# Forgetting bias of attention scores: fp32 products replaced by single-pass products of a rounded part and a rest, tables on Pool

## The chip, the cores and the metric

The kernel runs on one core of a Trainium2 chip. The metric is the device time of one launch in microseconds (us), the median of several runs. Every run computes the whole reference from inputs in HBM to outputs in HBM.

## The reference

One inference step of a two-layer encoder for 256 prompt tokens and 32 sample tokens, width 1024. Each layer is a SwiGLU block, a combined projection `z = h @ w_in` whose columns feed three head groups (forgetting attention, RWKV-7 mixing, retention), an output projection, a second SwiGLU block and a gated addition. The change touches forgetting attention (8 heads of 64):

```
c = cumsum(logf)                       # per head; for the sample over 512 cached + 32 new tokens
s = q k^T * 64**-0.5 + c[query] - c[key]
p = softmax(mask(s));  o = p v
```

The term `c[query] - c[key]` is the forgetting bias. It has to be exact to fp32 level, since the cached `logf` are large.

## The kernel before

All activations are feature-major (128 partitions are features, the free dimension is the 288 tokens). Weights come as 1 MB slots through a ring of four. Large products are made of operands split in two: a rounded part (type fp32r, made by ACT with a copy) and a rest (made by DVE with a subtraction, L844 and L930), and three single-pass products hi·hi, hi·lo, lo·hi. Small products in the mixers stay in fp32, which the trace records as two matmul records each.

There is one hand-written order per engine, joined by counting semaphores. In a layer: the first SwiGLU block; the z projection, 31 blocks of 24 products (`z_block`, L1465), for which ACT makes the rounded part (`z_cast`, L566) and DVE the rest (`z_rest`, L930) and the eviction of the block two before (`z_evict`, L939); `z_next(n)` is eviction n-2 and rest n. Between the z_next calls DVE does the small elementwise work of the mixers, in program order. Then come triangular solves and retention, and then attention and the RWKV recurrence interleaved: nine steps of the recurrence (L1769, L1775, L1782, with DVE's L1206 and L1213) and between them the attention of four head pairs (`fox_scores`, `fox_weights`, `fox_products`, `fox_back`). The sample's attention, the output projection and the second SwiGLU block follow.

The forgetting bias is part of the score product, as one more product into the same PSUM bank: `foxL` (weights, 128 rows x one column per head and query) times `foxR` (moving, 128 rows x 800 keys: 256 prompt, 512 cached, 32 new). Rows 0 to 7 of foxL hold 8·c of the query at the row of its head and rows 0 to 7 of foxR hold ones; rows 32 to 39 of foxL hold -8 at the row of the head (loaded once, L346) and rows 32 to 39 of foxR hold c of all keys; all other rows are zero. `fox_scores` (L1701) issues four such products per head pair, of 128 and 256 columns, and L1835 four for the sample, of 512 and 32 columns.

DVE makes c by scans over 8 partitions (L1057, L1058, L1060, multiplier: the ones of foxR), copies it to foxR (L1062, 8x800), and behind z_next(22) writes 8·c into foxL: one product of 8x2048 (L1064) and two of 8x128 (L1067), with broadcast operands. POOL issues loads of states and caches and stores of results, and makes a few elementwise products of RWKV's output stage (L440 to L443, L459, L460) while DVE works beside it. `cbuf`, where c stands, shares its memory with `tok`, which ACT writes after z (L644).

Of the kernel before, what the change touches and what calls it, by code (L numbers as in the profile page):

```python
# [19 lines left out]
F32 = mybir.dt.float32  # L20
# [59 lines left out]
for _name, _n in (("n1", DB), ("nm", DB), ("n2", DB), ("pn", DB), ("mu", 7), ("prev", 7), ("bf", 1), ("w0", 2),  # L80
# [27 lines left out]
    gn_ps=8, gn_sq=2, gn_ln=4, gn_rs=2, rot_ps=4, rotd=4, decd=2, rtr_ps=3, rtrc=3, sm_ps=6, smd=6, kv_ps=5,  # L108
    rsd=10, ro_ps=2, ro_ok=3, rgate=2, fu_ok=1, fl_ok=1, lgf_ok=1, fc_ok=3, vt_ps=3, vtc=3, fs_ps=8, fmx=16,
    fexp=16, ft_ps=8, ftc=8, fo_ps=4, fno=4, ft2=4, fo_ok=4, ss_ps=2, smx=2, sexp=4, st_ps=4, stc=4, so_ps=1,  # L110
# [19 lines left out]
def program(nc, wcol, x_in, p_in, consts_in, params_in, foxl_in, kc_in, vc_in, clf_in, srwkv_in, sret_in,  # L130
            nf_in, y_out, k_out, v_out, logf_out, shift_out, rwkv_out, ret_out):
    with ExitStack() as ctx:
        def sb(name, *shape):
            return ctx.enter_context(nc.sbuf_tensor(name, list(shape), F32))
# [18 lines left out]
        nf = sb("nf", P, DB)  # L153
        foxL = sb("foxL", P, FOX_H * T)
        foxLp = foxL[:, 0:FOX_H * TP].rearrange("p (h t) -> p h t", h=FOX_H)
        foxLs = foxL[:, FOX_H * TP:]
        foxR = sb("foxR", P, TP + PAST + TS)
        et = sb("et", P, 2, T)
# [170 lines left out]
        with nc.Block() as block:  # L329
            @block.sync  # L330
            def _(sp):
# [12 lines left out]
                sp.dma_start(nf[:], nf_in).then_inc(start_sem, 16)  # L344
                sp.wait_ge(clear_sem, 2)
                sp.dma_start(foxL[32:40, :], foxl_in).then_inc(start_sem, 16)  # L346

            @block.gpsimd
            def _(pool):
                pool.memset(foxL[:], 0.0).then_inc(clear_sem, 1)  # L350
                pool.memset(foxR[:], 0.0).then_inc(clear_sem, 1)
                pool.wait_ge(clear_sem, 2)
                pool.memset(foxR[0:8, :], 1.0).then_inc(clear_sem, 1)

# [9 lines left out]
        with nc.Block() as block:  # L364
# [41 lines left out]
            @block.gpsimd  # L406
            def _(pool):
                for layer in range(DEPTH):
                    past = counted(layer)
# [12 lines left out]
                    pool.dma_start(rst[:, 0, :, :], sret_in[layer, 0]).then_inc(S["ret_in"], 16)  # L422
                    pool.dma_start(rst[:, 5, :, :], sret_in[layer, 1]).then_inc(S["ret_in"], 16)

                    pool.wait_ge(S["z_ev"], past["z_ev"] + Z_BANKS + NZ)
# [41 lines left out]
            def _(act):  # L467
                n_chain = [0]
                for layer in range(DEPTH):
# [87 lines left out]
                    if layer == 0:  # L557
                        act.wait_ge(start_sem, 64)
                    def z_cast(n):
# [78 lines left out]

                    act.wait_ge(S["zstore"], layer * ZSTORE_PER_LAYER + 16)
                    for j in range(3):  # L640
                        n = TILES[j][1]
                        for k in range(2):
                            act.wait_ge(S["tr_ps"], past["tr_ps"] + 2 * j + k + 1)
                            act.activation(tok[0:n, j, 4 * k:4 * k + 4, :].rearrange("p a b -> p (a b)"),  # L644
                                           bank[6 + k][0:n, :], ACT.Copy).then_inc(S["trc"], 1)
# [171 lines left out]
            def _(dve):  # L817
                n_chain = [0]
                for layer in range(DEPTH):
                    past = counted(layer)  # L820

                    def link(ins):

                        n_chain[0] += 1
                        ins.then_inc(S["vchain"], 1)
                        dve.wait_ge(S["vchain"], n_chain[0])
# [94 lines left out]
                    if layer == 0:  # L921
                        dve.wait_ge(start_sem, 64)

# [125 lines left out]
                    for b in range(2):  # L1049
# [3 lines left out]
                    dve.wait_ge(S["mixin"], layer * MIXIN_PER_LAYER + 48)  # L1053
                    w = con[e8, CONSTS["fox8"][0]:CONSTS["fox8"][0] + 8]
                    unit = foxR[e8, :]
                    z_next(20)
# [4 lines left out]
                                                cbuf[e8, TP + PAST - 1:TP + PAST], ALU.mult, ALU.add))  # L1061
                    link(dve.tensor_copy(foxR[32:40, :], cbuf[e8, :]))  # L1062
                    z_next(22)
                    dve.tensor_tensor(foxLp[e8], cbuf[e8, 0:TP].unsqueeze(1).to_broadcast([8, FOX_H, TP]),  # L1064
                                      w.unsqueeze(2).to_broadcast([8, FOX_H, TP]), ALU.mult).then_inc(S["fc_ok"], 1)
                    for g in range(2):
                        dve.tensor_tensor(foxLs[e8, 128 * g:128 * g + 128].rearrange("p (b t) -> p b t", b=4),  # L1067
                                          cbuf[e8, TP + PAST:].unsqueeze(1).to_broadcast([8, 4, TS]),
                                          w.rearrange("p (b g) -> p g b", g=2)[:, g, :].unsqueeze(2).to_broadcast([8, 4, TS]),
                                          ALU.mult).then_inc(S["fc_ok"], 1)  # L1070
                    z_next(23)
# [270 lines left out]
            def _(pe):  # L1342
                for layer in range(DEPTH):
# [107 lines left out]
                    if layer == 0:  # L1451
                        pe.wait_ge(start_sem, 64)
                    def z_block(n):
# [237 lines left out]
                    pe.wait_ge(S["uac"], past["uac"] + 8)  # L1691
                    pe.wait_ge(S["fc_ok"], past["fc_ok"] + 3)

# [235 lines left out]
def constants():  # L1929
# [52 lines left out]
    put("dchunk", np.concatenate([np.exp(lg * 64.0), np.exp(lg * TS)], 1))  # L1982
    put("fox8", 8.0 * np.eye(8))
    cols = np.zeros((P, 8))
# [158 lines left out]
```

## Time and profile before

| | us |
|---|---|
| median of 3 runs | 1439.85 (1438.88 to 1444.85) |
| profiled execution | 1437.9 |
| its span | 1436.1 |
| PE busy in it | 1367.6 |
| DVE busy | 864.2 |
| ACT busy | 597.0 |
| POOL busy | 49.3 |

The profile is of one execution; the span is from its first to its last instruction. PE's matmul records overlap (the length of one is its latency, 0.29 us for 288 columns, while a new one starts every 0.13 us), so lengths of groups of them are read from one group's start to the next one's. Lines beginning with a time are of the timeline: start in us, duration in us, engine, line, operation, output<-inputs, shape, and how many were merged. The mean granted clock of TensorE over the span was 0.968 of 2.4 GHz.

### The profile page before, as it was taken

The numbers are of one execution on the slowest core, as the hardware profiler recorded it, in microseconds if no ns is written. First come the engines' busy times: TensorE is split into PE (matmuls) and PEld (weight loads), VectorE is DVE, ScalarE is ACT, GpSimd is POOL, SyncE is SP. The second block draws the span as 40 slices with busy tenths as digits, with TensorE's granted clock in tenths as the row PEclk, the third lists the DMA queues.
The fourth block names the chain that finished last, engine by engine and source line by source line (L and its number), as shares of the span: only waits on it lengthen the run. The fifth ranks groups of instructions, "written<-read, shape, count | busy, mean of one in ns | idle before, by whom it ended". The sixth has DMA issues, their size and how long they took to land.

```text
span 1436.1 us, 29222 instructions
## 1 busy us (share of the span) xinstructions
PE 1367.6 (95%) x12544; PEld 1317.7 (92%) x12544; DVE 864.2 (60%) x1365; ACT 597.0 (42%) x845; POOL 49.3 (3%) x71
## 2 busy tenths in 40 slices
PE   6999999998898999999999999999989899999997
PEld 6999999898777999999989999998977699999996
DVE  5766536796346566653766664467853565766546
ACT  5443434533326544433544343335333364443333
POOL 1000000003100000000000000000031100000000
PEclk9999999999779999999999999999997899999999
DMA  8444443434103344444444444523432035444440
GB/s 315 166 175 157 165 171 122 147 122 152 65 14 118 147 162 160 175 154 169 151 151 176 154 168 173 178 90 120 163 110 64 14 118 199 153 175 156 167 146 34
DMA packets 31328, 205.29 MB, mean 143 GB/s; under 512 B 4312, under 2 KB 5864, under 8 KB 7544
## 3 DMA queue, kind: packets, MB, share of 16 engines
q1 hardware_dynamic: 28672, 195.62, 37.9%
q0 software_dynamic: 2560, 8.26, 1.7%
q8 instruction: 75, 1.23, 0.3%
q14 instruction: 21, 0.17, 0.0%
HBM read 199.77 MB, written 4.10 MB: 142 GB/s over the span
## 4 chain that ended last, share of the span: by engine, by line
PE 88%; DVE 4%; ACT 4%; issue 2%; DMA 1%; POOL 0%; SPq 0%; DVEq 0%; ACTq 0%
PE banks L1390 40%; PE banks L1413 19%; PE banks L1465 11%; PE banks L1919 3%; PE banks L1882 3%; PE banks L1887 1%; PE banks L1701 1%; PE banks L1900 1%; PE banks L1743 1%; PE banks L1643 1%; PE banks L1821 1%; PE banks L1706 1%; ACT split_h L572 1%; PE banks L1631 1%; PE banks L1731 0%
## 5 line engine op out<-in xcount | busy, mean ns | idle before, releaser
L1390 PE MATMUL banks<-split_x,split_w 128*128 128x288 f32 x4224 | 570.5, 297 | 16.2 <-ACT split_x L492 11.8
L1390 PEld LDWEIGHTS banks<-split_x,split_w 128*128 128x128 f32 x4224 | 567.4, 190 | 18.8 <-issue 11.7
L844 DVE TENSOR_TENSOR split_w<-wc,split_w 128x2048 fp32r<-128x2048 f32 x139 | 318.6, 2292 | 346.5 <-ACT split_w L508 346.5
L508 ACT ACTIVATE split_w<-wc 128x2048 fp32r<-128x2048 f32 x139 | 266.4, 1916 | 401.0 <-PE banks L1390 207.4
L1413 PE MATMUL banks<-split_x,split_w 128*128 (+1 forms) x2112 | 282.3, 295 | 0.0
L1413 PEld LDWEIGHTS banks<-split_x,split_w 128*128 128x128 f32 x2112 | 281.8, 188 | 0.0
L1465 PE MATMUL banks<-split_h,split_x 128*128 128x288 f32 x752 | 115.7, 301 | 5.7 <-ACT split_x L566 4.2
L1465 PEld LDWEIGHTS banks<-split_h,split_x 128*128 128x128 f32 x752 | 105.9, 191 | 9.0 <-DVE zT L939 5.4
L566 ACT ACTIVATE split_x<-wc 128x1024 fp32r<-128x1024 f32 x62 | 65.1, 1057 | 112.2 <-PE banks L1465 97.2
L533 ACT ACTIVATE et<-hT 128x288 f32<-128x288 f32 x88 | 35.5, 445 | 110.4 <-DVE hT L863 110.3
L1465 PE MATMUL banks<-split_x 128*128 128x288 f32 x496 | 76.9, 298 | 0.0
L1465 PEld LDWEIGHTS banks<-split_x 128*128 128x128 f32 x496 | 70.2, 191 | 0.0
L1919 PE MATMUL banks<-split_x,split_w 128*128 128x288 f32 x384 | 53.0, 297 | 0.0
L1919 PEld LDWEIGHTS banks<-split_x,split_w 128*128 128x128 f32 x384 | 51.7, 189 | 1.1 <-ACT split_x L784 1.1
L939 DVE TENSOR_TENSOR zT<-banks,rs 128x288 f32<-128x288 f32 x62 | 28.1, 454 | 33.0 <-PE banks L1465 24.1
L1465 PE MATMUL banks<-split_h,split_e 128*128 128x288 f32 x240 | 38.2, 302 | 7.5 <-DVE split_e L930 7.5
L868 DVE SCALAR_TENSOR_TENSOR et<-et,hT 128x288 f32<-128x288 f32 x88 | 36.4, 455 | 12.6 <-ACT et L533 9.1
L930 DVE TENSOR_TENSOR split_x<-wc,split_x 128x1024 fp32r<-128x1024 f32 x32 | 39.0, 1218 | 7.8 <-ACT split_x L566 7.8
L874 DVE SCALAR_TENSOR_TENSOR et<-et,banks 128x288 f32<-128x288 f32 x88 | 39.3, 450 | 4.8 <-PE banks L1390 3.5
L1465 PEld LDWEIGHTS banks<-split_h,split_e 128*128 128x128 f32 x240 | 34.4, 193 | 8.4 <-DVE split_e L930 8.4
L930 DVE TENSOR_TENSOR split_e<-wc,split_x 128x1024 fp32r<-128x1024 f32 x30 | 36.5, 1217 | 6.8 <-ACT split_x L566 6.8
L863 DVE TENSOR_TENSOR hT<-banks,rs 128x288 f32<-128x288 f32 x88 | 35.9, 449 | 5.9 <-ACT rs L487 5.9
(290 smaller groups left out, 1194.6 us busy)
## 6 DMA issues: line engine op xcount, KB each, us to landing
wc<-wcol SPq DMA_DIRECT2D x182, 1024.0 KB, 4.8
arena<-kc_in POOLq DMA_DIRECT2D x8, 256.0 KB, 3.5
arena<-vc_in POOLq DMA_DIRECT2D x2, 1024.0 KB, 7.5
con<-consts_in SPq DMA_DIRECT2D x1, 1830.0 KB
xT<-x_in SPq DMA_DIRECT2D x2, 576.0 KB, 4.5
k_out<-zT POOLq DMA_DIRECT2D x8, 144.0 KB, 2.5
v_out<-zT POOLq DMA_DIRECT2D x8, 144.0 KB, 2.5
y_out<-hT SPq DMA_DIRECT2D x8, 144.0 KB, 1.9
```

The lines of the kernel that those rows point to most:

```text
L508: act.activation(ws[(s + 1 - f) % 2][0], wc[:, p % RING, :], ACT.Copy).then_inc(S["cast"], 1)
L566: act.activation(zw[n % 2][0], z_raw(n), ACT.Copy).then_inc(S["zcast"], 1)
L844: dve.tensor_tensor(lo, wc[:, (POS_FFN[f] + s) % RING, :], hi, ALU.subtract).then_inc(S["wlo"], 1)
L863: dve.tensor_tensor(half[:, q % 2, :], bank[2 * (q % 4)][:, 0:T], rs[:], ALU.mult)\
L868: dve.scalar_tensor_tensor(e, e, 1.0, half[:, q % 2, :], ALU.add, ALU.mult)\
L874: dve.scalar_tensor_tensor(e, e, 0.5, bank[2 * (q % 4) + 1][:, 0:T], ALU.mult, ALU.mult)\
L930: dve.tensor_tensor(lo, z_raw(n), hi, ALU.subtract).then_inc(S["zlo"], 1)
L1390: mm = pe.matmul(o, w[:, k, cs], x[:, k, :], start=(n == 0 and k == 0), stop=(n == 2 and k == DB - 1))
L1413: return pe.matmul(bank[m][:, 0:T], w[:, kk, m * 128:m * 128 + 128], rhs, start=start, stop=stop)
L1465: mm = pe.matmul(o, w[:, k, :], zh_lo(k) if second else zh_hi[:, k, :], start=(i == 0 and k == 0), stop=(i == 2 and k == DB - 1))
L1882: pe.matmul(bank[2 * s + cc][:, 0:T], hi[:, k, cc * 128:cc * 128 + 128], x[:, k, :], start=(x is oh_hi and k == 4), stop=False)
L1919: mm = pe.matmul(bank[2 * s + cc][:, 0:T], w[:, k, cc * 128:cc * 128 + 128], x[:, k, :], start=(n == 0 and k == 0), stop=(n == 2 and k == ...
```

## The change

c is split like the weights: a rounded part and a rest, both fp32r. foxL and foxR become fp32r tensors, so that the products on L1701 and L1835 are single-pass. Rows 0 to 7 and 64 to 71 of foxR hold the rounded part and the rest of c, against rows 0 to 7 and 64 to 71 of foxL with -8; rows 32 to 39 and 96 to 103 of foxR hold ones, against the rounded part and the rest times 8 in foxL. The number of products and their shapes stay.

DVE: the scans' multiplier is a broadcast constant column. The copy to foxR ahead of z_next(22) and the three products behind it go; in their place behind z_next(22) stand the rounding copy to foxR, the subtraction for the rest, and two copies of the parts to rows 32 and 96 of cbuf. POOL makes the tables of foxL from these, in two sets of one 8x2048 and two 8x128 products, between its loads of retention states and its stores of k and v; in the first launch part it also copies the -8 rows from a staging place to foxL after all constants are loaded.

```
-                sp.wait_ge(clear_sem, 2)
-                sp.dma_start(foxL[32:40, :], foxl_in).then_inc(start_sem, 16)
+                for r in (0, 64):
+                    sp.dma_start(extra[r:r + 8, 0:FOX_H * T], foxl_in).then_inc(start_sem, 16)
...
-                pool.memset(foxR[0:8, :], 1.0).then_inc(clear_sem, 1)
+                for r in (32, 96):
+                    pool.memset(foxR[r:r + 8, :].bitcast(F32), 1.0).then_inc(clear_sem, 1)
...
+                pool.wait_ge(start_sem, 80)
+                pool.wait_ge(clear_sem, 4)
+                for r in (0, 64):
+                    pool.tensor_copy(foxL[r:r + 8, :], extra[r:r + 8, 0:FOX_H * T]).then_inc(clear_sem, 1)
+                pool.wait_ge(clear_sem, 6)
...
+                    for i, r in enumerate((32, 96)):
+                        rows = slice(r, r + 8)
+                        w = c("fox8", rows)
+                        pool.wait_ge(S["fr_ok"], past["fr_ok"] + 3 + i)
+                        pool.tensor_tensor(foxLp[rows], cbuf[rows, 0:TP].unsqueeze(1).to_broadcast([8, FOX_H, TP]),
+                                           w.unsqueeze(2).to_broadcast([8, FOX_H, TP]), ALU.mult).then_inc(S["fc_ok"], 1)
+                        for g in range(2):
+                            pool.tensor_tensor(foxLs[rows, 128 * g:128 * g + 128].rearrange("p (b t) -> p b t", b=4),
+                                               cbuf[rows, TP + PAST:].unsqueeze(1).to_broadcast([8, 4, TS]),
+                                               w.rearrange("p (b g) -> p g b", g=2)[:, g, :].unsqueeze(2).to_broadcast([8, 4, TS]),
+                                               ALU.mult).then_inc(S["fc_ok"], 1)
+                    pool.wait_ge(S["fc_ok"], past["fc_ok"] + 6)
...
                     act.wait_ge(S["zstore"], layer * ZSTORE_PER_LAYER + 16)
+                    act.wait_ge(S["fc_ok"], past["fc_ok"] + 6)
...
-                    unit = foxR[e8, :]
+                    unit = col(C_ONE, e8).to_broadcast([8, PAST])
...
-                    link(dve.tensor_copy(foxR[32:40, :], cbuf[e8, :]))
                     z_next(22)
-                    dve.tensor_tensor(foxLp[e8], ...
-                    for g in range(2):
-                        dve.tensor_tensor(foxLs[e8, 128 * g:128 * g + 128]...
+                    dve.tensor_copy(foxR[e8, :], cbuf[e8, :]).then_inc(S["fr_ok"], 1)
+                    dve.wait_ge(S["fr_ok"], past["fr_ok"] + 1)
+                    dve.tensor_tensor(foxR[64:72, :], cbuf[e8, :], foxR[e8, :], ALU.subtract).then_inc(S["fr_ok"], 1)
+                    dve.tensor_copy(cbuf[32:40, :], foxR[e8, :]).then_inc(S["fr_ok"], 1)
+                    dve.wait_ge(S["fr_ok"], past["fr_ok"] + 2)
+                    dve.tensor_copy(cbuf[96:104, :], foxR[64:72, :]).then_inc(S["fr_ok"], 1)
                     z_next(23)
...
-                    pe.wait_ge(S["fc_ok"], past["fc_ok"] + 3)
+                    pe.wait_ge(S["fr_ok"], past["fr_ok"] + 2)
+                    pe.wait_ge(S["fc_ok"], past["fc_ok"] + 6)
```

The waits on the start semaphore count to 80 in place of 64, and the constant `fox8` stands at rows 32 and 96.

## Rows read from the trace of the kernel before

**Rows 1.** The page: busy times of the engines, and the chain's shares by engine.
```profile
PE 1367.6 (95%) x12544; PEld 1317.7 (92%) x12544; DVE 864.2 (60%) x1365; ACT 597.0 (42%) x845; POOL 49.3 (3%) x71
...
PE 88%; DVE 4%; ACT 4%; issue 2%; DMA 1%; POOL 0%; SPq 0%; DVEq 0%; ACTq 0%
```
**Rows 2.** Timeline of PE, z stage of layer 0.
```profile
314.14 1.23 PE L1465 MATMUL banks<-split_h,split_e 128*128 128x288 f32 x8
...
317.34 1.23 PE L1465 MATMUL banks<-split_h,split_x 128*128 128x288 f32 x8
...
323.17 1.32 PE L1465 MATMUL banks<-split_h,split_e 128*128 128x288 f32 x8 [1.52 <-DVE split_e L930]
```
**Rows 3.** Timeline of DVE, the same stretch.
```profile
306.44 0.57 DVE L1062 COPY foxR<-extra 8x800 f32<-8x800 f32 x1
...
308.55 2.27 DVE L1064 TENSOR_TENSOR foxL<-extra,con 8x2048 f32<-8x2048 f32 x1
...
310.75 0.47 DVE L1067 TENSOR_TENSOR foxL<-extra,con 8x128 f32<-8x128 f32 x2
...
311.52 1.20 DVE L930 TENSOR_TENSOR split_e<-wc,split_x 128x1024 fp32r<-128x1024 f32 x1
...
314.16 0.76 DVE L1081 TENSOR_TENSOR zT<-zT,et 128x576 f32<-128x576 f32 x1
```
**Rows 4.** Timeline of POOL over the span.
```profile
2.68 0.76 POOL L351 MEMSET foxR<- 128x800 f32 x1
3.51 0.75 POOL L353 MEMSET foxR<- 8x800 f32 x1
...
348.40 1.68 POOL L441 TENSOR_TENSOR arena<-arena 128x576 f32<-128x576 f32 x1
...
433.98 1.40 POOL L459 TENSOR_TENSOR arena<-arena 128x576 f32<-128x576 f32 x1 [8.21 <-ACT arena L728]
```
**Rows 5.** Lines 1114 and 1115: ns min/median/max, first and last start in us.
```profile
L1114 DVE TENSOR_TENSOR hT<-zT,con x2: 744/748/751, 348.1 to 1059.3; 128x576 f32<-128x576 f32 x2
...
L1115 DVE TENSOR_TENSOR hT<-zT,con x2: 1949/1956/1964, 348.8 to 1060.0; 128x576 f32<-128x576 f32 x2
```
**Rows 6.** Chain of waits in layer 0's attention: start us, us, what.
```profile
378.24 2.86 PE banks L1701 x8
...
388.27 1.31 PE banks L1701 x8
...
395.21 0.66 PE banks L1731 x6
...
405.33 1.28 PE banks L1731 x6
406.61 2.56 PE banks L1701 x8
...
429.05 2.54 PE banks L1835 x8
```
**Rows 7.** Windows of 2 us: length, PE busy (records), clock, DMA share, GB/s.
```profile
380.00:382.00 2.00, 2.00 (x10) 0.50 0.94 371
382.00:384.00 2.00, 1.80 (x30) 0.99 0.18 72
```
**Rows 8.** z stages: PE timeline and windows (layer 1); PE waits, whole-stage window (0).
```profile
944.11 1.30 PE L1465 MATMUL banks<-split_h,split_x 128*128 128x288 f32 x8 [2.10 <-ACT split_x L566]
...
944.00:946.00 2.00, 1.89 (x12) 0.81 0.00 0
946.00:948.00 2.00, 2.00 (x10) 0.50 0.28 49
948.00:950.00 2.00, 2.00 (x15) 0.83 0.84 336
...
PE banks L1465 <- DVE split_e L930: 3.8, 2, 2.2
...
204.00:342.00 138.00, 130.78 (x995) 127.07 (x998) 97.51 (x147) 59.16 (x85) 2.69 (x5) 1.00 0.41 146
```

More of the change, by code:

```diff
@@ L108 @@
     gn_ps=8, gn_sq=2, gn_ln=4, gn_rs=2, rot_ps=4, rotd=4, decd=2, rtr_ps=3, rtrc=3, sm_ps=6, smd=6, kv_ps=5,
-    rsd=10, ro_ps=2, ro_ok=3, rgate=2, fu_ok=1, fl_ok=1, lgf_ok=1, fc_ok=3, vt_ps=3, vtc=3, fs_ps=8, fmx=16,
+    rsd=10, ro_ps=2, ro_ok=3, rgate=2, fu_ok=1, fl_ok=1, lgf_ok=1, fr_ok=4, fc_ok=6, vt_ps=3, vtc=3, fs_ps=8, fmx=16,
     fexp=16, ft_ps=8, ftc=8, fo_ps=4, fno=4, ft2=4, fo_ok=4, ss_ps=2, smx=2, sexp=4, st_ps=4, stc=4, so_ps=1,
@@ L153, in program @@
         nf = sb("nf", P, DB)
-        foxL = sb("foxL", P, FOX_H * T)
+        foxL = ctx.enter_context(nc.sbuf_tensor("foxL", [P, FOX_H * T], F32R))
         foxLp = foxL[:, 0:FOX_H * TP].rearrange("p (h t) -> p h t", h=FOX_H)
         foxLs = foxL[:, FOX_H * TP:]
-        foxR = sb("foxR", P, TP + PAST + TS)
+        foxR = ctx.enter_context(nc.sbuf_tensor("foxR", [P, TP + PAST + TS], F32R))
         et = sb("et", P, 2, T)
@@ L344, in _ @@
                 sp.dma_start(nf[:], nf_in).then_inc(start_sem, 16)
-                sp.wait_ge(clear_sem, 2)
-                sp.dma_start(foxL[32:40, :], foxl_in).then_inc(start_sem, 16)
+                for r in (0, 64):
+                    sp.dma_start(extra[r:r + 8, 0:FOX_H * T], foxl_in).then_inc(start_sem, 16)
             @block.gpsimd
             def _(pool):
-                pool.memset(foxL[:], 0.0).then_inc(clear_sem, 1)
-                pool.memset(foxR[:], 0.0).then_inc(clear_sem, 1)
+                pool.memset(foxL[:].bitcast(F32), 0.0).then_inc(clear_sem, 1)
+                pool.memset(foxR[:].bitcast(F32), 0.0).then_inc(clear_sem, 1)
                 pool.wait_ge(clear_sem, 2)
-                pool.memset(foxR[0:8, :], 1.0).then_inc(clear_sem, 1)
+                for r in (32, 96):
+                    pool.memset(foxR[r:r + 8, :].bitcast(F32), 1.0).then_inc(clear_sem, 1)
             @block.scalar
@@ L557, in _ @@
                     if layer == 0:
-                        act.wait_ge(start_sem, 64)
+                        act.wait_ge(start_sem, 80)
                     def z_cast(n):
@@ L921, in _ @@
                     if layer == 0:
-                        dve.wait_ge(start_sem, 64)
+                        dve.wait_ge(start_sem, 80)
+                        dve.wait_ge(clear_sem, 6)
                     def z_rest(n):
@@ L1053, in _ @@
                     dve.wait_ge(S["mixin"], layer * MIXIN_PER_LAYER + 48)
-                    w = con[e8, CONSTS["fox8"][0]:CONSTS["fox8"][0] + 8]
-                    unit = foxR[e8, :]
+                    unit = col(C_ONE, e8).to_broadcast([8, PAST])
                     z_next(20)
@@ L1061, in _ @@
                                                 cbuf[e8, TP + PAST - 1:TP + PAST], ALU.mult, ALU.add))
-                    link(dve.tensor_copy(foxR[32:40, :], cbuf[e8, :]))
                     z_next(22)
-                    dve.tensor_tensor(foxLp[e8], cbuf[e8, 0:TP].unsqueeze(1).to_broadcast([8, FOX_H, TP]),
-                                      w.unsqueeze(2).to_broadcast([8, FOX_H, TP]), ALU.mult).then_inc(S["fc_ok"], 1)
-                    for g in range(2):
[L1067 to L1070, printed above, removed]
+                    dve.tensor_copy(foxR[e8, :], cbuf[e8, :]).then_inc(S["fr_ok"], 1)
[4 more added lines that the diff above has]
+                    dve.tensor_copy(cbuf[96:104, :], foxR[64:72, :]).then_inc(S["fr_ok"], 1)
                     z_next(23)
@@ L1451, in _ @@
                     if layer == 0:
-                        pe.wait_ge(start_sem, 64)
+                        pe.wait_ge(start_sem, 80)
                     def z_block(n):
@@ L1982, in constants @@
     put("dchunk", np.concatenate([np.exp(lg * 64.0), np.exp(lg * TS)], 1))
-    put("fox8", 8.0 * np.eye(8))
+    fox8 = np.zeros((P, 8))
+    fox8[32:40] = fox8[96:104] = 8.0 * np.eye(8)
+    put("fox8", fox8)
     cols = np.zeros((P, 8))
```

## The prediction

> **What bounds the kernel now.** I read the page's busy shares and its chain first. The reader is to see that PE is busy 95% of the span and carries 88% of the chain that ended last [rows 1]: time is won or lost where PE's stream shortens or has to wait. The change touches three stretches of each layer, so the second view is the timeline there: PE and DVE in the z projection (one block of 24 products per 3.2 us, 314.14 to 317.34), where DVE makes the rests that PE consumes [rows 2, 3]; the 36 us in which POOL works beside DVE [rows 4, 5]; and the attention stretch from 378 us, where every group of fox products is a link of the chain [rows 6]. The last view is the granted clock by windows of 2 us [rows 7, 8], because the attention stretch runs at 1.2 and at 2.4 GHz by turns.
>
> **Scores on PE.** Four groups of four fp32 products per layer become four groups of four single-pass ones. A product of 128 or 256 columns is now two records. At full clock a group takes 1.31 us; at half clock 2.86 and 2.56 us [rows 6]. Single-pass records of 128x128 (the transposes) take 0.66 / 6 = 0.11 us at full clock and 1.28 / 6 = 0.21 us at half [rows 6]. So a new group costs about 4 x 0.11 to 0.12 = 0.47 us at full and 0.88 us at half. Per layer this removes 2 x 0.84 (groups two and three) + 1.98 + 1.68 = 5.3 us. The sample's products, 2.54 us partly at half clock [rows 6], have 2 x (512 + 32) columns; the two wide ones become 2 x 0.23 us by the z products' rate (3.2 us / 24 = 0.133 us for 288 columns [rows 2], in proportion), the narrow ones 0.11 each: 0.7 us, so 1.5 us less on the mean of the layers (less where the clock is full). Together 6.8 us a layer. What follows is late instead: after the second group PE meets ACT's copies and DVE's maxima, which start only when the scores are there and move along with them, but not all; I take 85%, 5.8 us a layer, 11.6 us in both. Bounds: nothing on records that are narrower than 288 columns, if the single pass needs wide operands, to the full 13.6 us.
>
> **Clock of that stretch.** The clock came back to 2.4 GHz at 382 us, right behind the first score group and the products after it, and it is at half through 380 to 382 although PE was busy all the time [rows 7]; by the fourth group, at 406.61 us, it had fallen again, since that took 2.56 us where the second took 1.31 [rows 6]. The dense four-pass products are what stands ahead of the rise. With a quarter of their array time the rise may come later or not at all, and the fall sooner. By the transposes' 0.66 against 1.28 us [rows 6], PE's own work doubles; of the some 30 us of the stretch that have full clock, PE would lose up to 10 us in a layer (a third; the rest is overhead, waits and the other engines). Ends: 0 and 10 us a layer. I take the middle, 5 us a layer, 10 us in all, since the trace shows no such stretch without the dense products. The Trainium skill (TensorE: Matmul & The Clock Gate, Part 4: PE-mode transpose) says that transposes do not count as PE work for the clock. No row here separates them; by that rule it would be the transposes that cannot stand in for the scores, and the loss would be the upper end, 20 us.
>
> **DVE in the z stage.** Removed behind z_next(22): 2.27 + 0.47 us, and the copy of 0.57 us ahead of it [rows 3]. Added: three copies of 8x800 at 0.57 us and a subtraction of 800 columns at 2.27 / 2048 = 1.11 ns each, 0.89 us: 2.6 us against 3.3. Were the rounding copy at one column per such step, 0.3 us more. DVE is not late by this: rest(23), which ended at 312.72 us (311.52 + 1.20 [rows 3]), is needed by PE at 314.14 us [rows 2]. The scan's multiplier becomes a repeated constant column: no price either way. Alone this part is worth 0.
>
> **The tables on POOL, and what they hold up.** POOL gets, twice per layer, one product of 8x2048 and two of 8x128. POOL's 128x576 product with nobody in its way took 1.40 us; a memset of 8x800 took as long as one of 128x800, 0.75 and 0.76 us [rows 4], so few partitions don't help. Less some 0.1 us of start, that is 2.26 ns a column, 4.7 us for 2048, 0.4 us for 128. By 1.40 / 576 it would be 5.0 us. The Trainium skill (GPSIMD Engine Reference, 3.1 Elementwise) gives 4.5 us for 2048 columns; the sum would be 0.4 us a layer lower. POOL's deadline is far (PE reads the tables at 378 us, ACT overwrites their source behind z), so its own time costs nothing. What it does to DVE does. L1114 and L1115 are the same operation, 128x576 with two operands in SBUF: 0.75 us and 1.95 us, in both layers [rows 5]. The second met POOL's L441, 348.40 to 350.08 us [rows 4], started at 348.8 us and ended 0.62 us behind it, at 350.70. So a DVE operation with two SBUF operands stood still until POOL's two-operand product was through. DVE's rests (L930) are of that kind.
>
> Layer 0 in the new order (times from the rows of the stage, [rows 2, 3]): scan to 306.4, z_next(22) to 308.1, round 308.7, subtract 309.65, copy 310.25 (this frees POOL), copy 310.85, POOL's first long product 310.9 to 315.5. DVE's eviction reads one operand from PSUM and goes on; rest(23) waits and ends at 315.5 + 1.1 = 316.6. PE wants it at 314.14: 2.4 us of stall. POOL's short ones and DVE's L1078, L1079 interleave to about 318.1; the second long product takes 318.1 to 322.8 and holds L1081; the eviction, a short POOL product and rest(24) follow, to 325.1 us. PE wants rest(24) at 317.34 + 2.4 = 319.75: 5.4 us of stall. The stall of 1.52 us before 323.17 stays, since it hangs on the rotation behind block 24 [rows 2]. Sum 7.8 us per layer, 15.6 us in all. Lower bound 0 (operations on 8 partitions may not hold DVE), upper 2 x 10 us (slower POOL product for the repeated operands). Idle PE also costs clock: behind a gap of 2.10 us in layer 1's z stage three windows show 0.81, 0.50 and 0.83, which is (0.19 + 0.50 + 0.17) x 2 / 0.5 = 3.4 us at half, while layer 0 had two waits of that size (3.8 us together) and kept 1.00 [rows 8]. A gap of 5.4 us I expect to cost one such spell per layer, 1.7 us, 3.4 us in all (0 to 7).
>
> **Cheap edits.** Start: one memset more (0.75 us [rows 4]) and one DMA more on SP, whose wait for the memsets goes; both end inside the 9 us until the first weights are there. The copies of 8x2304 on POOL come after the constants have landed, some 20 us in, and could hold DVE's rest of 2.3 us per weight slot for 2 to 5 us each; DVE is busy 60% [rows 1], so I take 0, and 2 us if PE waits for one. They also stand ahead of POOL's loads of states and cached gates, which are needed 280 us later. New waits: ACT's for the tables is behind z, 15 us after they are ready; POOL's stands ahead of the stores of k and v, whose data come last in z; PE's is met. 0.
>
> **Sum.** Against the profiled execution, 1437.9 us: + 15.6 (stalls) + 3.4 (clock there) - 11.6 (scores) + 10 (clock in attention) = 1455.3 us. The median of the runs shown, 1439.85, lies 2 us higher: 1457 us.
>
> **Rivals.** (1) POOL holds DVE, but the clock in attention stays as it is: 1439.85 + 15.6 + 1.7 - 11.6 = 1445.6 us, hardly to be told from before. For it: the clock kept 1.00 through other stretches of small products; against: both rises stand behind score groups. (2) POOL doesn't hold DVE, because it touches 8 partitions: then the gain stands, 1439.85 - 11.6 = 1428 us, or 1438 us with half of the clock lost; this is the one on the other side. It decides if rest(23) and L1081 keep 1.20 and 0.76 us beside POOL. For it: no row shows an 8-partition product beside DVE; against: L1115 in both layers. (3) Both losses at their full size, clock at half through attention: 1439.85 + 15.6 + 3.4 - 11.6 + 20 = 1467 us. (4) The single pass isn't one at 128 and 256 columns: the gain is 3 us (the sample's wide products alone) instead of 11.6, but the clock in attention stays: 1439.85 + 15.6 + 3.4 - 3 = 1456 us. Every single-pass product of this trace has 288 columns, which neither speaks for it nor against.
>
> **Chances.** Forecast 0.43 (own range 1448 to 1466), rival one 0.20, two 0.25, three 0.08, four 0.04. Within 0.5% of 1439.85 (1432.7 to 1447.0) is about what measurement can't tell from no change. Slower: all of three and four, nearly all of the forecast and a quarter of rival one, 0.58. Same: most of rival one and the part of rival two with clock lost, 0.27. Faster: 0.15. The range reaches from rival two's middle to rival three, 1432 to 1468 us.
>
> **What would show it.** POOL's long products should take 4.5 to 5 us; rest(23) and L1081 5 us instead of about 1; PE should show two waits for L930 or L1081 of 2 to 6 us in each z stage, followed by a half-clock window; score groups of 4 records in 0.5 us; fewer full-clock windows from 378 to 420 us. I am wrong if DVE's operations beside POOL keep their lengths, or if the attention stretch keeps its clock and the net falls under 1447 us.

## The result and the profile after

| | before | after |
|---|---|---|
| median of 4 runs each, us | 1439.76 (1438.88 to 1444.85) | 1454.68 (1450.57 to 1460.71) |
| profiled execution, us | 1437.9 | 1450.57 |
| its span | 1436.1 | 1449.0 |
| PE busy | 1367.6 | 1376.7 |
| PE records | 12544 | 12504 |
| granted clock | 0.968 | 0.952 |

The ratio is 1.0087, 95% interval 1.0055 to 1.0119: slower by 0.9%, 2.3 us less than forecast. Timed a second time, beside other kernels, the changed kernel had 1.0075 (1.0047 to 1.0102). Ratios leave out slow runs, those more than 1.5% above the fastest of their kernel: one of 6 in that second timing, one of 12 with memsets (whose profile is of that run), 4 of 12 with filler in the gaps. PE is busy 9 us longer with fewer records, which is the first sign of a lower clock. From the page of the profile after: busy times, chain shares, and a group of DVE's rests, whose mean of 1413 ns hides long ones:

```profile
PE 1376.7 (95%) x12504; PEld 1326.7 (92%) x12504; DVE 876.5 (60%) x1365; ACT 597.6 (41%) x845; POOL 77.7 (5%) x86
...
PE 87%; DVE 6%; ACT 3%; issue 2%; DMA 1%; POOL 0%; SPq 0%; DVEq 0%; ACTq 0%; POOLq 0%
...
L951 DVE TENSOR_TENSOR split_e<-wc,split_x 128x1024 fp32r<-128x1024 f32 x30 | 42.4, 1413 | 6.8 <-ACT split_x L585 6.8
```

The z stage of layer 0. POOL's timeline (start us, us, engine, line, operation, shape, count, idle before it):

```profile
313.50 3.97 POOL L435 TENSOR_TENSOR foxL<-extra,con 8x2048 fp32r<-8x2048 f32 x1 [3.44 <-DVE extra L1086]
317.45 1.73 POOL L438 TENSOR_TENSOR foxL<-extra,con 8x128 fp32r<-8x128 f32 x2
319.25 4.17 POOL L435 TENSOR_TENSOR foxL<-extra,con 8x2048 fp32r<-8x2048 f32 x1
323.39 1.28 POOL L438 TENSOR_TENSOR foxL<-extra,con 8x128 fp32r<-8x128 f32 x2
```

DVE beside it; L951 and L1099 answer to L930 and L1081 of [rows 3]:

```profile
311.24 0.56 DVE L1083 CAST foxR<-extra 8x800 fp32r<-8x800 f32 x1
311.83 0.98 DVE L1085 TENSOR_TENSOR foxR<-extra,foxR 8x800 fp32r<-8x800 f32 x1
...
314.05 0.46 DVE L960 TENSOR_TENSOR zT<-banks,rs 128x288 f32<-128x288 f32 x1
314.42 4.14 DVE L951 TENSOR_TENSOR split_e<-wc,split_x 128x1024 fp32r<-128x1024 f32 x1
...
319.21 0.74 DVE L1097 TENSOR_TENSOR zT<-zT,con 128x576 f32<-128x576 f32 x1
319.99 4.05 DVE L1099 TENSOR_TENSOR zT<-zT,et 128x576 f32<-128x576 f32 x1
...
324.45 1.30 DVE L951 TENSOR_TENSOR split_x<-wc,split_x 128x1024 fp32r<-128x1024 f32 x1
```

The rest that took 1.20 us in [rows 3] takes 4.14, and L1081's 0.76 has become 4.05. Each ends about its own length behind POOL's long product: 318.56 against 317.47, 324.04 against 323.42. The eviction of 0.46 us, which reads one operand from PSUM, ran beside the same product at its own length. So did L1097, 0.74 us, with two operands in SBUF: it started 0.04 us before the second long product, so it had come first. The waits that this makes on PE, from PE's timeline:

```profile
318.61 1.32 PE L1483 MATMUL banks<-split_h,split_e 128*128 128x288 f32 x8 [1.16 <-DVE split_e L951]
325.80 1.42 PE L1483 MATMUL banks<-split_h,split_x 128*128 128x288 f32 x8 [3.74 <-DVE split_x L951]
332.78 1.32 PE L1483 MATMUL banks<-split_h,split_e 128*128 128x288 f32 x8 [0.95 <-DVE split_e L951]
```

And windows behind the longest of these waits (us, PE busy, PEld busy, DVE, ACT, POOL, clock, DMA share, GB/s):

```profile
326.00:328.00 2.00, 2.00 (x11) 1.71 (x11) 0.00 (x0) 0.69 (x1) 0.00 (x0) 0.71 0.03 8
328.00:330.00 2.00, 2.00 (x8) 1.71 (x7) 1.28 (x3) 0.36 (x1) 0.00 (x0) 0.50 0.00 0
330.00:332.00 2.00, 1.83 (x13) 1.59 (x11) 1.93 (x4) 0.00 (x0) 0.00 (x0) 0.93 0.00 0
```

The attention stretch of layer 0: the chain of the profile after, whose groups of 4 records answer to those of 8 in [rows 6]:

```profile
388.12 1.15 PE banks L1720 x4
...
398.69 0.85 PE banks L1720 x4
...
408.11 1.28 PE banks L1750 x6
409.39 0.85 PE banks L1720 x4
...
420.69 0.85 PE banks L1720 x4
...
440.39 0.59 PE banks L1854 x4
```

Groups two to four are as short as promised for half clock; the first takes 1.15 us. But the transposes beside the third group take 1.28 us where the ones at full clock took 0.66, and none of the four groups ran at full clock throughout (in layer 1 the second did). Windows of 72 us over this stretch, before and then after; the clock, third from the end, falls from 0.83 to 0.67:

```profile
378.00:450.00 72.00, 62.80 (x780) 49.80 (x777) 36.58 (x106) 28.98 (x69) 4.41 (x5) 0.83 0.11 38
```

```profile
388.00:460.00 72.00, 66.15 (x757) 53.83 (x754) 36.11 (x106) 29.36 (x69) 4.42 (x5) 0.67 0.10 33
```

Both profiled executions were laid side by side between fixed points of PE's stream. "Half" is the time at 1.2 GHz in the stretch.

| stretch | layer 0 before | after | layer 1 before | after |
|---|---|---|---|---|
| z block 22 to block 26 | 15.52 (half 0) | 21.98 (3.4) | 15.53 (0) | 21.78 (3.4) |
| first scores to end of recurrence | 37.19 (10.7) | 40.03 (31.0) | 37.35 (10.9) | 37.25 (21.2) |
| on to the sample's products | 13.49 (9.2) | 11.94 (6.8) | 8.11 (0) | 7.54 (0) |
| on to the output projection | 14.41 (1.0) | 13.53 (7.2) | 14.08 (4.2) | 13.14 (6.0) |

z: +6.5 and +6.3, 12.7 us. Attention: +0.4 and -1.6, -1.2 us. The first z product starts 1.6 us later (226.44 before, 227.99 after); kernels below with the same start have 226.4 to 227.4, so at least half of this is scatter. Other stretches nearly cancel: blocks 0 to 21 of z +1.6 and -1.6 us (a half-clock spell more in one layer, one less in the other), the stretch ahead of the first scores +0.3 and -1.8, and all behind the attention +1.4. Sum 13.0; the span grew by 12.9.

### The profile page after: what moved, and what is told of

Read it like the earlier page. It is cut to its first block, busy times and chain, and to the rows that moved or that the text cites. A ratio compares the mean times of both kernels' runs of the same rounds, so it can differ in the third digit from the quotient of the medians.

```text
span 1449.0 us, 29161 instructions
## 1 busy us (share of the span) xinstructions
PE 1376.7 (95%) x12504; PEld 1326.7 (92%) x12504; DVE 876.5 (60%) x1365; ACT 597.6 (41%) x845; POOL 77.7 (5%) x86
## 4 chain that ended last, share of the span: by engine, by line
PE 87%; DVE 6%; ACT 3%; issue 2%; DMA 1%; POOL 0%; SPq 0%; DVEq 0%; ACTq 0%; POOLq 0%
PE banks L1408 39%; PE banks L1431 19%; PE banks L1483 9%; PE banks L1938 3%; PE banks L1901 3%; PE banks L1906 1%; PE banks L1919 1%; PE banks L1762 1%; DVE split_e L951 1%; PE banks L1725 1%; DVE split_x L951 1%; DVE zT L1099 1%; PE banks L1661 1%; PE banks L1840 1%; PE banks L1788 1%
## 5 line engine op out<-in xcount | busy, mean ns | idle before, releaser
L1408 PE MATMUL banks<-split_x,split_w 128*128 128x288 f32 x4224 | 571.6, 298 | 16.7 <-ACT split_x L511 12.3
L1483 PEld LDWEIGHTS banks<-split_h,split_x 128*128 128x128 f32 x752 | 107.4, 194 | 17.4 <-DVE split_x L951 9.4
L951 DVE TENSOR_TENSOR split_e<-wc,split_x 128x1024 fp32r<-128x1024 f32 x30 | 42.4, 1413 | 6.8 <-ACT split_x L585 6.8
L951 DVE TENSOR_TENSOR split_x<-wc,split_x 128x1024 fp32r<-128x1024 f32 x32 | 39.2, 1224 | 7.9 <-ACT split_x L585 7.8
```

Source lines behind the costliest of these rows:

```text
L951: dve.tensor_tensor(lo, z_raw(n), hi, ALU.subtract).then_inc(S["zlo"], 1)
L1408: mm = pe.matmul(o, w[:, k, cs], x[:, k, :], start=(n == 0 and k == 0), stop=(n == 2 and k == DB - 1))
L1483: mm = pe.matmul(o, w[:, k, :], zh_lo(k) if second else zh_hi[:, k, :], start=(i == 0 and k == 0), stop=(i == 2 and k == DB - 1))
```

## Experiments

Ratios are to the kernel before, timed beside it on the same chip, with 95% intervals. One number is used throughout beside the time: **half-clock time** = (1 - mean granted clock) x 2 x span, mean over the runs that the ratio uses. The kernel before has 99 to 106 us of it in its timings, the changed one 148 (4 runs) and 138 (second timing, 5 runs). It scatters: over the 12 runs of one kernel it reached from 124 to 183 us, so that a mean over 12 has a standard error of 3 to 6 us. "First stretch of attention" is the second stretch of the table above, in the one profiled execution of a kernel.

**The tables on DVE, late in z.**

```
-POOL: two sets of one 8x2048 and two 8x128 products
+                        if n > 26:                 # DVE, behind z_next(27) to z_next(30)
+                            table((32, 32, 96, 96)[n - 27], (0, 4, 0, 4)[n - 27])   # 8x1024 each
+                    table_s(32); table_s(96)       # 8x128, before the last evictions
```

> The changed kernel with the tables of foxL made by DVE in place of POOL, in four products of 8x1024 behind z_next(27) to z_next(30) and four of 8x128 before the last evictions, where DVE has idle time. Theory (POOL's two-operand products hold DVE's two-operand ones in the z stage, and the rest of the change about cancels): blocks 22 to 26 of z take 15.5 us again instead of 21.8, rest(23) 1.2 us, the attention stretch as in the changed kernel, 1438 to 1442 us. Rival (the loss comes from the clock of the attention stretch): blocks 22 to 26 may recover, but the time stays at 1450 us or more.

1442.48 us against 1442.66, ratio 0.9996 (0.9964 to 1.0028). The z stretch is back at 15.52 us in both layers. Its table products on DVE, and the rests beside them:

```profile
329.33 1.22 DVE L939 TENSOR_TENSOR split_e<-wc,split_x 128x1024 fp32r<-128x1024 f32 x1
330.58 1.22 DVE L1094 TENSOR_TENSOR foxL<-extra,con 8x1024 fp32r<-8x1024 f32 x1
...
332.32 1.22 DVE L939 TENSOR_TENSOR split_x<-wc,split_x 128x1024 fp32r<-128x1024 f32 x1
```

This is the theory's result, 0.5 us above its range. DVE can do all of this work for nothing, and with it on POOL the kernel loses 0.8 to 0.9%. It also shows what the single-pass scores alone are worth: nothing, though PE has less to do. Half-clock time is 146 us, 40 more than before. The first stretch of attention took 37.3 us (half 21.3) and 39.7 (30.3).

**POOL's long product in eight pieces.**

```
+                        for h in range(FOX_H):
+                            pool.tensor_tensor(foxLp[rows, h, :], cbuf[rows, 0:TP],
+                                               w[:, h:h + 1].to_broadcast([8, TP]), ALU.mult)...
```

> The changed kernel with POOL's product of 8x2048 cut into eight of 8x256, one per head. Theory (a DVE operation stands still until the POOL product that is running is through, and gets in before the next one): no DVE operation waits more than 0.7 us, rest(23) takes 1.2 to 1.9 us, blocks 22 to 26 of z take 15.5 to 17 us, 1440 to 1444 us. Rival (POOL's reads and DVE's share the port's rate, so the sum of POOL's work counts): blocks 22 to 26 stay near 21.8 us, 1452 to 1456 us.

1442.53 us, ratio 1.0004 (0.9984 to 1.0024); z stretch 16.18 and 17.10 us. POOL, then DVE:

```profile
312.55 8.11 POOL L436 TENSOR_TENSOR foxL<-extra,con 8x256 fp32r<-8x256 f32 x8 [3.42 <-DVE extra L1087]
```

```profile
313.48 1.21 DVE L952 TENSOR_TENSOR split_e<-wc,split_x 128x1024 fp32r<-128x1024 f32 x1
...
315.34 1.01 DVE L1098 TENSOR_TENSOR zT<-zT,con 128x576 f32<-128x576 f32 x1
316.38 1.05 DVE L1100 TENSOR_TENSOR zT<-zT,et 128x576 f32<-128x576 f32 x1
```

POOL works twice as long (8.11 us where one product took 3.97), on the same data, and DVE loses at most 0.4 us per operation (0.3 in the lines shown). Blocks 22 to 26 came out 0.1 us above the theory's range in layer 1. The hold is by instruction, not by amount of traffic. It goes both ways. Two of POOL's pieces, one beside DVE's next rest and the next one alone:

```profile
317.84 1.21 DVE L952 TENSOR_TENSOR split_x<-wc,split_x 128x1024 fp32r<-128x1024 f32 x1
317.87 1.66 POOL L436 TENSOR_TENSOR foxL<-extra,con 8x256 fp32r<-8x256 f32 x1
...
319.49 0.60 POOL L436 TENSOR_TENSOR foxL<-extra,con 8x256 fp32r<-8x256 f32 x1
```

The rest, which started 0.03 us earlier, keeps its 1.21 us, and the piece ends 0.47 us behind it. So most of the added time of POOL is its waiting for DVE: alone, eight pieces would take 4.8 us (8 x 0.60, an estimate). What the cutting leaves of the loss in z, 0.7 and 1.6 us, is within the interval of the ratio.

**POOL's products replaced by memsets of the same places**, from which the query's part of the bias is missing.

```
-                        pool.tensor_tensor(foxLp[rows], cbuf[rows, 0:TP]... , ALU.mult)
+                        pool.memset(foxL[rows, :].bitcast(F32), 0.0)     # twice, then foxLs
```

> The changed kernel with POOL's products for foxL replaced by memsets of 8x2304 and 8x256 (twice 2.0 us and 0.3 us per set), so the query's part of the bias is left out. Theory (only a POOL operation that reads SBUF holds DVE's second operand): rest(23) and L1099's operation keep 1.2 and 0.76 us beside POOL, blocks 22 to 26 take 15.5 us, 1438 to 1442 us. Rival (any POOL work on SBUF holds DVE): rest(23) takes 2 to 4 us, blocks 22 to 26 17 to 20 us, 1443 to 1450 us.

1443.57 us, ratio 1.0001 (0.9975 to 1.0027); z stretch 16.54 and 16.52 us, where the theory had 15.5. POOL and DVE:

```profile
312.87 2.02 POOL L434 MEMSET foxL<- 8x2304 f32 x1 [3.54 <-DVE extra L1083]
314.95 2.34 POOL L436 MEMSET foxL<- 8x2304 f32 x1
```

```profile
312.85 2.48 DVE L1085 COPY extra<-foxR 8x800 f32<-8x800 f32 x1
...
315.73 1.22 DVE L948 TENSOR_TENSOR split_e<-wc,split_x 128x1024 fp32r<-128x1024 f32 x1
```

The rest beside a memset keeps 1.22 us; DVE's plain copy beside the first memset takes 2.48 us instead of 0.57 and ends 0.44 us behind it. The theory had left this copy out; it pushes the rests behind it back, and z is 1 us longer. The Trainium skill (SBUF — State Buffer, "Who interferes with whom") states both sides: a DVE instruction with two SBUF inputs contends with a GpSimd instruction that reads, not with one that only writes, while a copy in a two-port mode contends with either, and who comes first holds the shared ports for its whole instruction. The four pairs here agree: 4.14 us beside a product, 1.22 beside a memset, 2.48 for a copy beside a memset, 0.46 for an operation with one operand in PSUM beside a product. On who comes first, L1097 and the rest beside POOL's piece agree, each the earlier by 0.03 to 0.04 us; the copy held by the memset has the earlier start in the trace, by 0.02 us, which is too close to tell.

**The change with fp32 tables and scores**, all else as changed.

```
-        foxL = ctx.enter_context(nc.sbuf_tensor("foxL", [P, FOX_H * T], F32R))
+        foxL = sb("foxL", P, FOX_H * T)              # foxR likewise
```

> The changed kernel with foxL and foxR in fp32, so that the products stay fp32 ones (the rounded part is then all of c, the rest zero), all else as in the change. Theory: blocks 22 to 26 still take 21 to 22 us, the attention stretch is as before with 1.31 us per score group at full clock, and half-clock time there near 11 us a layer: 1453 to 1458 us. Rival (the single-pass products and their clock cost the time): 1440 to 1444 us.

1457.63 us, ratio 1.0096 (1.0071 to 1.0121). z is again 22.5 us, and the first stretch of attention 37.13 us (half 10.6) and 38.45 (12.5), as before the change. The clock of the attention stretch thus follows the kind of the score products, not the tables on POOL or the stalls in z.

**Less work still: no query part, no tables at all** (the query part left out, the copies and the waits too).

```
-                    dve.tensor_copy(cbuf[32:40, :], foxR[e8, :])...
-                    dve.tensor_copy(cbuf[96:104, :], foxR[64:72, :])...
-                    (POOL's products and the waits on them)
```

> The changed kernel without the query's part of the bias: no tables, neither on POOL nor on DVE, and without the two copies to rows 32 and 96, so the bias is -c of the key alone (the query's part is constant along a row of the softmax). Theory: blocks 22 to 26 take 15.5 us, as with late tables, attention as there, 1438 to 1443 us; the tables' DVE time was hidden. Rival (DVE's 6 us of late tables cost something at the end of z): 2 to 5 us faster than the version with late tables.

1441.81 us, ratio 1.0003 (0.9979 to 1.0028), half-clock time 139 us, z stretch 15.51 us: not the 2 to 5 us less of the rival. Whatever makes the tables, single-pass scores alone bring nothing.

**The changed kernel again.**

> The changed kernel itself once more, beside the others on the same chip. Theory: blocks 22 to 26 of z take 21 to 22 us in both layers, 1453 to 1458 us, 0.9 to 1.0% above the kernel before. Rival (the first measurement was high by the spread of the clock): 1446 to 1450 us.

1454.47 us, ratio 1.0075 (1.0047 to 1.0102). z stretch 22.43 and 22.53 us. First stretch of attention: 37.37 us (half 21.4) and 36.06 (19.0), against 40.03 (31.0) and 37.25 (21.2) in the first profile: the clock there is not the same from run to run.

**Filler in the first score group** (tables on DVE): its 128x256 single-pass product issued 7 times per head.

```
-                            for q, k1, at in parts:
+                            for q, k1, at in (7 if p == 0 else 1) * parts[1:] + parts[:1]:
```

> The version with late DVE tables, and in the first score group of each layer the 128x256 product of each head is issued seven times in place of once (twelve more products, each starting the sum anew, so the result is the same). Theory (dense products ahead of a rise bring the clock back, and the single-pass scores lack that density): the clock rises within 4 us of the first group, half-clock time from there to the end of the recurrence falls from 21 to 30 us to 11 to 17, and the stretch, 2.5 us of added products included, takes 36 to 37 us instead of 37.3 to 39.7; total 1438 to 1442 us. Rival (the clock follows something else, or the phase alone): half-clock time stays at 21 us or more, the stretch gets 2.5 us longer, total 1444 to 1450 us.

1442.69 us median (one of 12 runs took 2600.61, which nothing here explains), ratio 0.9999 (0.9981 to 1.0017). First stretch of attention 37.2 us in both layers with 16.7 half, the group 3.40 us long. It bought clock, half-clock time 125 instead of the 139 of the kernel without tables beside it, and paid as much for it: the time came out a little above the theory's range, the ratio at 1.

**Filler in the gaps** (tables on DVE): three unused 128x256 products ahead of each wait of PE in the recurrence.

```
+                        for _ in range(3):
+                            pe.matmul(bank[2][:, 256:512], foxLp[:, 0, 0:128], foxR[:, 0:256], ...)
```

> The version with late DVE tables, and in each of the nine recurrence steps three 128x256 single-pass products into unused columns of PSUM stand ahead of PE's wait for DVE's update, where PE idles some 0.2 to 0.6 us. Theory (what raises the clock and holds it is the density of PE's array work): half-clock time from the first scores to the end of the recurrence falls under 10 us per layer and the stretch takes 35 to 37 us instead of 37.3 to 39.7; total 1434 to 1440 us. Rival (the clock does not follow it): half-clock time stays above 20 us, the stretch gets up to 4 us longer, total 1446 to 1450 us.

1443.37 us is the median of all 12 runs (1426.97 to 1459.61), above the 1441.34 of the kernel before; the ratio, 0.9964 (0.9933 to 0.9994), is of 8 of them. In the profile layer 0 had 32.1 us of half clock in the first stretch of attention and layer 1 had 9.5. Inconclusive.

**Which dense group matters.** The tables on DVE; chosen score groups read the same rounded tables as fp32, the rest single-pass. Three kernels, `p == 0`, `p in (0, 3)` and `p == 3`:

```
+                                lhs, rhs = foxLp[:, 2 * p + e, q:q + 128], foxR[:, 0:k1]
+                                if p in (0, 3):
+                                    lhs, rhs = lhs.bitcast(F32), rhs.bitcast(F32)
```

> The tables are made by DVE late in z, and the first score group of each layer reads the same rounded tables as fp32 (8 records), the other three and the sample's as single-pass products. Theory (the dense four-pass products of the first group bring the clock's rise): half-clock time from the first scores to the end of the recurrence back at 10 to 13 us a layer, as with all four groups in fp32, where one with four single-pass groups has 21 to 30; the second and third groups take 0.7 us at full clock; that stretch 34 to 36 us instead of 37.2, time 1434 to 1439 us where before has 1441 (ratio 0.995 to 0.998). Rival (the rise and fall do not hang on that group): half-clock time 20 to 31 us in at least one layer, stretch 37 to 40 us, ratio 0.998 to 1.002.

> As the last, but the first and the fourth score group of each layer in fp32, the second and third and the sample's single-pass. Theory (dense products keep the clock up): half-clock time 8 to 12 us a layer, stretch from the first scores to the end of the recurrence 34.5 to 36.5 us, ratio 0.995 to 0.999. Rival (they do not): half-clock time 20 us or more in a layer, the fourth group adds 1.6 us at half clock, ratio 0.999 to 1.003.

> The tables on DVE late in z, all score groups single-pass, timed beside the two others. Theory: 0.998 to 1.001 of before as in its first run (0.9996), with half-clock time of 20 to 30 us a layer; the ratio lies above that of the kernel with its first group in fp32. Rival: all three kernels within 0.1% of each other.

> Tables on DVE late in z; of the four score groups of a layer only the fourth in fp32. Half-clock time is counted as (1 - granted clock) x 2 x span, mean over the timed runs: 106 us for the kernel before, 146 with four single-pass groups, 135 with only the first in fp32, 108 with the first and the fourth. Theory one (the fourth group, where the clock falls, is what decides): half-clock time 105 to 120 us, ratio 0.993 to 0.997. Theory two (both are needed: the clock follows the work of the whole stretch): 125 to 140 us, ratio 0.998 to 1.002. Rival (any fp32 group only costs its own array time and the clock is scatter): 146 us as with none, ratio 1.001 to 1.003.

| groups in fp32 | median us (before beside it) | ratio | half-clock time | half clock in first stretch of attention, layers 0 and 1 of the profile |
|---|---|---|---|---|
| none | 1443.20 (1442.86) | 0.9999 (0.9972 to 1.0026) | 145 | 39.7, 35.3 (first profile 21.3, 30.3) |
| first | 1442.87 (1442.86) | 1.0010 (0.9983 to 1.0038) | 135 | 8.3, 16.2 |
| fourth | 1442.11 (1442.13) | 0.9990 (0.9966 to 1.0013) | 133 | 28.6, 30.9 |
| first and fourth | 1435.60 (1442.86) | 0.9958 (0.9942 to 0.9975) | 108 | 7.6, 8.9 |
| before (all, tables in fp32) | 1442.86 | 1 | 106 | 10.7, 10.9 |

12 runs of each of the first four; the one with the fourth group was timed apart from the others. My theory of the single cause, that the dense products of the first group bring the rise and so the time back, fell: alone they give back 10 us of half clock, the fourth group alone 12, both together 37. With standard errors of 3 to 6 us on each mean, neither group alone does what both do. That the two together do more than the sum of each (37 against 22) is suggested and not shown: resampling the runs puts the difference between -3 and 32 us. The last column, one execution each, has the theory right for the first stretch alone: with the first group in fp32 it is short of half clock, with the fourth alone it isn't. Over whole runs that did not pay.

The chain of the kernel with both in fp32, layer 0:

```profile
381.68 2.86 PE banks L1729 x8
...
398.20 0.66 PE banks L1759 x6
398.85 0.46 PE banks L1729 x4
...
407.07 1.28 PE banks L1759 x6
408.35 2.04 PE banks L1729 x8
```

The third group, at 398.85 us, takes 0.46 us at full clock here against 0.85 in the changed kernel. Whole cores, the changed kernel and this one:

```profile
core 0: 1449.0 us, clock 0.952
```

```profile
core 0: 1432.3 us, clock 0.965
```

This version is the only one clearly faster than both: 0.4% below before, 1.2% below the change (by the two ratios, 0.9958 / 1.0075 = 0.988). Its control, tables late on DVE with all four groups in fp32, was not run, so the 0.4% is not split between the scores and the moved tables.

## Why the prediction was right, step by step

**DVE's own part: right, worth nothing.** The four operations behind z_next(22) took 2.8 us (311.24 to 314.02) for 2.6 forecast, and with the tables off POOL blocks 22 to 26 were back at 15.52 us.

**Tables on POOL hold DVE: right in kind, too large.** Stalls and clock were put at 9.5 us a layer; 6.5 and 6.3 were measured in the profile, 6.9 and 7.0 in the second one. Counted from the start of block 22 (308.81 us before, 311.96 after), the working shows where it was off. POOL was to start behind the second copy, at +2.1; it started behind the first, at +1.5. Its product ended 3.97 us later, not 4.7. So the rest ended at +6.6 instead of +7.8: 1.2 us of the 2.4 us stall gone, 1.16 left. Between the long products lay 1.8 us, not 2.6, and the second took 4.17: the second rest ended at +13.8, not +16.3, while PE, less late itself, wanted it at +10.1, not +10.9: 3.7 us, not 5.4. And the old stall of 1.52 us before block 25 did not stay: 0.95. That is 4.3 us of stalls in place of 7.8, and 1.7 for the clock spell, which came in both layers as forecast (3.4 us at half); some 0.5 us of the 6.5 is left over. For the price of POOL's product I had 4.7 us by [rows 4]; by the Trainium skill (GPSIMD Engine Reference, 3.1 Elementwise) it is 4.5; 3.97 to 4.17 was measured, on 8 partitions, so both were high. Even these hold a wait: each product started 0.04 to 0.05 us behind a DVE operation, which went on for 0.52 and 0.70 us. Less that, both are about 3.5 us, an estimate of the product's price alone.

**Scores on PE: right.** Groups went from 8 records to 4, 0.85 us at half clock (0.88 forecast) and 0.46 at full (0.47; from the chain just shown, since the profile of after has no group at full clock in layer 0). The sample's first four now take 0.59. That single-pass products are single at 128 and 256 columns is thereby shown, and rival four is out.

**Clock of attention: right in sign and amount, the price a little low.** The loss was put at 10 us. The profile cannot give it by itself, since two profiles of the same kernel differ by 2.7 us in one stretch. The timed runs can, with an assumption: with the tables on DVE, half-clock time is 40 us above before (146 against 106, give or take 12) and the time is level. Inside one kernel, the 12 runs of that version spread from 1435.65 to 1456.0 us, and a straight line through their times rises by 0.32 us per us of half clock (0.25 to 0.34 in the other kernels with 11 or 12 runs in their ratio, 0.27 to 0.33 in before beside them). That line is a correlation. If it is a price and holds from kernel to kernel too, which is an estimate, the clock costs 40 x 0.32 = 13 us (10 to 14 by the slopes alone), and the gain on PE that it cancels is as large, against 11.6 forecast. The forecast had taken 10 us a layer as the loss if all of some 30 us at full clock went to half; these would become 40 us, so it priced half-clock time at 0.25 us per us, and its middle, 5 us a layer, stands for some 20 us of it a layer, 40 in all. That is the amount measured. Taking the middle between 0 and 10 was a choice without a row behind it, so that the amount came out is luck in good part. With the first and fourth group in fp32, half-clock time is +2 us and the time 6 to 7 us under before (by the ratio and by the medians). By the prediction's own terms two groups of 0.84 and 1.5 us for the sample are 3.2 us a layer, 6.4: it fits.

**Net.** Forecast +17.4 us on the profiled execution (15.6 + 3.4 - 11.6 + 10), measured +12.7: z 12.7 for 19.0, attention -1.2 for -1.6, 1.6 at the start for 0. The last is not of the change, as far as the scatter of that point tells. In the second profile of the change, attention from the first scores to the output projection is 3.3 us shorter in layer 0 and 5.0 us longer in layer 1 than in the first, so the close -1.2 is chance too. And the medians come within 2.3 us of the forecast because that of the changed kernel lies 4.1 us above its profiled execution, where the one before lies 1.9 above: by the two ratios the change costs 11 to 12.5 us, for 17 forecast. The term that was mis-sized is z, by 6.3 us.

**Cheap edits: right, with one seen.** POOL's two copies at the start (6.2 us together, from 23.76 us) lengthened one of DVE's rests from 2.29 to 3.08 us; PE did not wait for it.

Of the rivals, one (clock unaffected, 1445.6 us) is refuted by the clock: 0.952, and 138 to 148 us at half. Two (POOL doesn't hold DVE) is refuted by the 4.14 us. Its form with half of the clock lost, 1438 us, is 4.5 us under what the tables on DVE gave when nothing held DVE: 1442.5. Three (half clock all through attention, 1467 us) is refuted by the time and by the profile after, where the first stretch had 31.0 of 40 us at half in layer 0 and 21.2 of 37 in layer 1. The sum for rival one has 1.7 us for the clock in z, where the forecast itself had 3.4.

**Open.** What makes the clock fall and rise at a given moment of the attention stretch is not settled. Shown is that single-pass score products in it raise the half-clock time by 40 us, that neither the first nor the fourth group in fp32 does alone what both do (10, 12, together 37), and that the same kernel spreads by 20 us between runs with it. Which single-pass group would be the best to keep was tried for three choices only. How much of the transposes' work counts was not tried.

## What to carry to other kernels

Work moved to an idle POOL is not free for DVE: look for DVE operations with two SBUF operands, or plain copies, that run beside it and have less slack than POOL's longest instruction; if it must be POOL, cut it into short instructions. Cheaper PE products in a stretch where PE waits often may be paid back through a lower granted clock; compare half-clock time over many runs before and after, not one profile, and try keeping part of the dense work where its removal gains least. A change of two independent parts should be timed apart: here one was worth 0 and the other cost 0.9%.

## What the runs showed of the hardware that was not expected

- The hold between POOL and DVE goes both ways and ends with each instruction: a POOL product of 8x256 takes 0.60 us alone and 1.66 when it starts 0.03 us behind a DVE rest of 1.21. That, and not the cutting, is most of why eight of them took 8.11 us where one of 8x2048 took 3.97.
- A memset of 8x2304 on POOL (2.02 us) stretched a DVE copy of 8x800 from 0.57 to 2.48 us; a DVE subtraction with two SBUF operands kept its 1.22 us beside another.
- Single-pass score products save half the records (8 to 4) and two thirds of a group's time (1.31 to 0.46 us at full clock).
- Most of the scatter between runs of one kernel goes with the clock: correlation of time and half-clock time 0.96 over 12 runs with the tables on DVE (1435.65 to 1456.0 us), 0.94 over 29 runs of before beside it (1438.37 to 1454.95); 0.69 over the 29 of before in the second timing of the change, which spread less (1435.04 to 1446.51).
